# Stick-breaking attention of a trunk kernel: the next pair's scores ahead of head A's values, fillers divided about both, and suffix sums of all heads from running sums over key blocks

## What is computed

```python
z = jnp.einsum('bhqd,bhkd->bhqk', qi, k).astype(jnp.float32) * scale
strict = key_pos[None, :] < q_pos[:, None]
log_1m = jnp.where(strict, jax.nn.log_sigmoid(-z), 0.0)
tail = lax.cumsum(log_1m, axis=3, reverse=True) - log_1m
a = jnp.where(strict, jnp.exp(jax.nn.log_sigmoid(z) + tail), 0.0)
return jnp.einsum('bhqk,bhkd->bhqd', a.astype(v.dtype), v)
```

## Time and profile before

| what | value |
|---|---|
| median of three runs | 748.08 us (746.58 to 751.45) |
| the profiled execution | 748.02 us, of which the span is 746.3 us |
| busy: PE, DVE, ACT | 694.2 us (93%), 520.1 us (70%), 404.6 us (54%) |
| mean granted clock of PE | 0.978 of full speed |
| the eight heads' suffix sums and values | from 110.45 to 196.18 us |

### The profile page before, as it was taken

The page is one execution under the profiler, slowest core; times in us unless marked ns, Lnnn a source line. Parts: engine busy times, 40 slices in busy tenths (PEclk is TensorE's granted clock), DMA queues, the critical chain, the costliest instruction groups (busy, mean ns, idle before and its releaser), DMA issues.

```text
span 746.3 us, 9922 instructions
## 1 busy us (share of the span) xinstructions
PE 694.2 (93%) x3547; PEld 579.3 (78%) x3547; DVE 520.1 (70%) x567; ACT 404.6 (54%) x416; POOL 109.5 (15%) x112
## 2 busy tenths in 40 slices
PE   4999999999999999999999989999999999999920
PEld 3798889788888888888889758888888888888810
DVE  5868775868607062350745679999999999999927
ACT  6726674567414032221503337777777777777712
POOL 5000000000000000000000140333333333331120
PEclk9999999999999999999999999999999999999975
DMA  8662321000052332332592379999999999999344
GB/s 270 190 170 57 113 74 40 4 25 15 30 162 77 113 98 74 119 103 91 191 364 116 141 277 393 396 386 372 362 379 375 375 373 364 372 376 373 156 183 183
DMA packets 85169, 155.47 MB, mean 208 GB/s; under 512 B 6229, under 2 KB 37071, under 8 KB 84628
## 3 DMA queue, kind: packets, MB, share of 16 engines
q1 hardware_dynamic: 78452, 137.39, 52.2%
q0 software_dynamic: 6688, 17.69, 6.2%
HBM read 150.64 MB, written 12.58 MB: 219 GB/s over the span
## 4 chain that ended last, share of the span: by engine, by line
PE 86%; DVE 7%; ACT 3%; issue 2%; DMA 2%; POOL 1%; POOLq 0%; DVEq 0%; ACTq 0%
PE ps L483 25%; PE ps L485 24%; PE ps L484 24%; PE ps L1520 2%; PE ps L1265 1%; PE ps L1267 1%; PE ps L1446 1%; PE ps L1577 1%; PE ps L1546 1%; PE ps L1474 1%; PE ps L1303 1%; DMA y_rows<-ye,y_col 1%; DMA y_in<-y_rows 1%; DVE x L2162 1%; DVE soft_lo L1817 1%
## 5 line engine op out<-in xcount | busy, mean ns | idle before, releaser
L456 DVE TENSOR_TENSOR ring_lo<-raw_a,ring_hi 128x2048 fp32r<-128x2048 f32 (+2 forms) x58 | 115.5, 1995 | 95.8 <-ACT ring_hi L450 95.8
L456 DVE TENSOR_TENSOR ring_lo<-raw,ring_hi 128x2048 fp32r<-128x2048 f32 x71 | 161.4, 2290 | 12.3 <-ACT ring_hi L450 11.0
L450 ACT ACTIVATE ring_hi<-raw 128x2048 fp32r<-128x2048 f32 x71 | 136.3, 1920 | 19.8 <-PE ps L485 19.8
L483 PE MATMUL ps<-hT_hi,ring_hi 128*128 128x512 f32 x288 | 113.6, 394 | 2.1 <-DVE hT_lo L1667 1.8
L450 ACT ACTIVATE ring_hi<-raw_a 128x2048 fp32r<-128x2048 f32 (+2 forms) x58 | 97.4, 1680 | 32.4 <-PE ps L485 32.2
L485 PE MATMUL ps<-hT_hi,ring_lo 128*128 128x512 f32 x288 | 112.2, 390 | 0.0
L484 PE MATMUL ps<-hT_lo,ring_hi 128*128 128x512 f32 x288 | 112.2, 390 | 0.0
L483 PE MATMUL ps<-ring_hi,xT_hi 128*128 128x512 f32 x240 | 94.8, 395 | 1.8 <-DVE xT_lo L2020 1.8
L485 PE MATMUL ps<-ring_hi,xT_lo 128*128 128x512 f32 x240 | 93.8, 391 | 0.0
L484 PE MATMUL ps<-ring_lo,xT_hi 128*128 128x512 f32 x240 | 93.6, 390 | 0.0
L483 PEld LDWEIGHTS ps<-hT_hi,ring_hi 128*128 128x128 f32 x288 | 54.1, 188 | 14.4 <-DVE ring_lo L1662 1.2
(11 more groups left out here) (344 smaller groups left out, 1215.8 us busy)
## 6 DMA issues: line engine op xcount, KB each, us to landing
raw<-in_w_down SPq DMA_DIRECT2D x25, 1024.0 KB
raw<-in_w_gate SPq DMA_DIRECT2D x47, 512.0 KB
raw<-in_w_up SPq DMA_DIRECT2D x47, 512.0 KB
raw_a<-in_w_in SPq DMA_DIRECT2D x15, 1024.0 KB
raw_a<-in_w_gate SPq DMA_DIRECT2D x17, 512.0 KB
raw_a<-in_w_up SPq DMA_DIRECT2D x17, 512.0 KB
raw_a<-in_w_down SPq DMA_DIRECT2D x7, 1024.0 KB
raw_a<-in_w_in SPq DMA_DIRECT2D x10, 512.0 KB, 8.2
```

The source lines that it names most:

```text
L450: act.activation(ring_hi[:, c[0] % SPLIT, 0:width], buf[:, 0:width], ACT.Copy).then_inc(hi_ready, 1)
L456: dve.tensor_tensor(ring_lo[:, s, 0:width], buf[:, 0:width], ring_hi[:, s, 0:width].bitcast(F32), ALU.subtract).then_inc(lo_ready, 1)
L483: pe.matmul(out_ap, l_hi, r_hi, start=start, stop=False, skip_group_check=True)
```

## The change

**PE.** `tails` goes only over a key block's own block and the next one, 7 pairs, 14 matmuls. The next block is met by a new constant `negrest`, -1 where `negtri` is 0. The order becomes: `tails(A)`, three quarters of `fill_a`, `tails(B)`, the last quarter, scores of the next pair, `values(A)`, half of `fill_b`, `values(B)`, the other half. The last pair is written out apart from the loop. **DVE.** After `softplus` three additions, each linked to the one before it, add the strip of block `sbk+1` to that of `sbk`, for 2, 1 and 0: 128, 256 and 384 columns. `softplus(B+2)` now stands ahead of `value_sum(B)` and `qk_lo`. **ACT.** The Abs is a step of its own (`magnitude`), `weigh(B)` goes ahead of the copy of `fill_a`'s result, the Abs of A+2 ahead of `value_x(A)`, and the three steps of B+2 follow at once on those of A+2. `negrest` lies where `gain_rows` lay, which is read once at the start.

The diff, cut to its core:

```diff
+    negrest = sb("negrest", [P, P], F32R, "const", cursor["const"] - 512)
...
+        SUMMED = tuple(range(HEADS))
...
+            def magnitude(n):
+
+                act.wait_ge(z_ps, n + 1)
+                act.activation(soft[n % 2][:, :], scores(n), ACT.Abs).then_inc(act_c, 1)
+
             def logarithm(n):
 
-                act.wait_ge(z_ps, n + 1)
                 buf = soft[n % 2]
-                act.activation(buf[:, :], scores(n), ACT.Abs).then_inc(act_c, 1)
                 act.wait_ge(act_c, 2 * n + 1)
...
             for p in range(HEADS // 2):
                 a, b = 2 * p, 2 * p + 1
                 weigh(a)
+                if p in (1, 2):
+                    split_hi(act, K(C_MERGE + p - 1))
+                weigh(b)
                 if p == 0:
                     v_hi_part(2, 6)
                 if p == 1:
                     qk_hi(6, 6)
-                    split_hi(act, K(C_MERGE))
                 if p == 2:
                     v_hi_part(3, 6)
-                    split_hi(act, K(C_MERGE + 1))
-                weigh(b)
+                if p < HEADS // 2 - 1:
+                    magnitude(a + 2)
                 value_x(a)
                 if p < HEADS // 2 - 1:
                     logarithm(a + 2)
+                    magnitude(b + 2)
+                    logarithm(b + 2)
                 value_x(b)
                 if p == 0:
                     qk_hi(5, 6)
                 if p == 1:
                     qk_hi(7, 6)
-                if p < HEADS // 2 - 1:
-                    logarithm(b + 2)
                 value_hi(a)
                 value_hi(b)
...
-                    pe.wait_ge(consts_r, 3)
+                    pe.wait_ge(consts_r, 4)
...
                 for sbk in range(TB):
-                    for jb in range(sbk, TB):
+                    end = min(sbk + 2, TB) if n in SUMMED else TB
+                    for jb in range(sbk, end):
                         o = ZOFF[sbk] + (jb - sbk) * P
                         j, w = ZOFF[jb], ZN[jb]
-                        lhs = negtri if jb == sbk else negones
+                        lhs = negtri if jb == sbk else negrest if n in SUMMED else negones
...
-            for p in range(HEADS // 2):
+            for p in range(HEADS // 2 - 1):
                 tails(2 * p)
-                fill_a(p)
+                fill_a(p, 0, 6)
                 tails(2 * p + 1)
+                fill_a(p, 6, KD)
+                scores_pair(p + 1)
                 values(2 * p)
-                if p < HEADS // 2 - 1:
-                    scores_pair(p + 1)
-                    fill_b(p, 0, CUT)
-                else:
-                    gate_half(0, 1, 0, None, 5, KD).then_inc(chunk_used, 1)
+                fill_b(p, 0, 4)
                 values(2 * p + 1)
-                if p < HEADS // 2 - 1:
-                    fill_b(p, CUT, KD)
+                fill_b(p, 4, KD)
+            tails(HEADS - 2)
+            pe.wait_ge(av_sum, HEADS - 2)
+            gate_half(0, 1, 0, None, 0, 5)
+            tails(HEADS - 1)
+            values(HEADS - 2)
+            gate_half(0, 1, 0, None, 5, KD).then_inc(chunk_used, 1)
+            values(HEADS - 1)
...
+            dve.tensor_scalar(negrest[:, :], tri_f[:, :], -1.0, -1.0, ALU.mult, ALU.add).then_inc(consts_r, 1)
...
             def softplus(n):
                 dve.wait_ge(z_ln, n + 1)
-                dve.scalar_tensor_tensor(soft[n % 2][:, :], bank(3 * (n % 2), 3)[:, 0:ZW], 0.0, soft[n % 2][:, :],
-                                         ALU.max, ALU.add).then_inc(z_soft, 1)
+                buf = soft[n % 2]
+                ins = dve.scalar_tensor_tensor(buf[:, :], bank(3 * (n % 2), 3)[:, 0:ZW], 0.0, buf[:, :],
+                                               ALU.max, ALU.add)
+                if n in SUMMED:
+                    for sbk in (2, 1, 0):
+                        link(ins)
+                        more = buf[:, ZOFF[sbk] + P:ZOFF[sbk] + ZN[sbk]]
+                        ins = dve.tensor_tensor(more, more, buf[:, ZOFF[sbk + 1]:ZOFF[sbk + 1] + ZN[sbk + 1]], ALU.add)
+                ins.then_inc(z_soft, 1)
...
                 weight_hi(b)
                 value_sum(a)
                 weight_lo(b)
-                if p == HEADS // 2 - 1:
-                    dve.sem_inc(b_used, 3)
-                if p < HEADS // 2 - 1:
-                    softplus(a + 2)
-                    soft_split(a + 2)
+                softplus(a + 2)
+                soft_split(a + 2)
+                softplus(b + 2)
                 value_sum(b)
                 if p == 0:
                     qk_lo(5, 6)
                 if p == 1:
                     qk_lo(7, 6)
-                if p < HEADS // 2 - 1:
-                    softplus(b + 2)
                 value_lo(a)
                 value_lo(b)
```

More of the change, by code:

```diff
@@ L925, in value_hi @@
                 act.activation(sbT_hi[rows, m // 2, :], sbT_f[rows, m // 2, :], ACT.Copy).then_inc(av_h, 1)
+            magnitude(0)
             logarithm(0)
@@ L931, in _ @@
             cross_o(1)
+            magnitude(1)
             logarithm(1)
@@ L1197, in project_qk, with project_v @@
                     ins.then_inc(chunk_used if n % 2 else q_ps, 1)
-            def project_v(i, b):
+            def project_v(i, b, s0=0, s1=2 * KD):
                 wh, wl = chunk(K(C_V[i // 2]))
-                for u in range(2):
+                for step in range(s0, s1):
+                    u, k = step // KD, step % KD
                     t = 2 * (i % 2) + u
[L1204 to L1208, removed]
+                    ins = three(pe, bank(b)[:, u * 256:(u + 1) * 256], hT_hi[:, k, t * P:(t + 1) * P],
+                                hT_lo[:, k, t * P:(t + 1) * P], wh[:, k * 256:(k + 1) * 256],
+                                wl[:, k * 256:(k + 1) * 256], k == 0, k == KD - 1)
+                if s1 == 2 * KD:
+                    ins.then_inc(chunk_used if i % 2 else v_ps, 1)
             cross_scores(0)
@@ L1267, in tails @@
                         ins = pe.matmul(zz[:, o:o + w], lhs[:, :], soft_lo[n % 2][:, j:j + w], start=False,
-                                        stop=jb == TB - 1, skip_group_check=True)
+                                        stop=jb == end - 1, skip_group_check=True)
                 ins.then_inc(tail_ps, 1)
@@ L1326, in _, with fill_a @@
             project_qk(4, 6)
-            CUT = 2
-            def fill_a(p):
+            def fill_a(p, k0, k1):
                 if p == 0:
                     pe.wait_ge(qk_l, 5)
-                    project_v(2, 6)
+                    project_v(2, 6, 2 * k0, 2 * k1)
                 if p == 1:
                     pe.wait_ge(qk_l, 6)
-                    project_qk(6, 6)
+                    project_qk(6, 6, k0, k1)
                 if p == 2:
                     pe.wait_ge(qk_l, 8)
[L1338 to L1341, removed]
+                    project_v(3, 6, 2 * k0, 2 * k1)
             def fill_b(p, k0, k1):
@@ L1848, in _ @@
                 weight_lo(a)
+                if p in (1, 2):
+                    split_lo(dve, K(C_MERGE + p - 1))
                 if p == 0:
@@ L1869, in _ @@
                     qk_lo(7, 6)
-                if p < HEADS // 2 - 1:
-                    softplus(b + 2)
                 value_lo(a)
                 value_lo(b)
+            a, b = HEADS - 2, HEADS - 1
+            soft_split(b)
+            weight_hi(a)
+            weight_lo(a)
+            weight_hi(b)
+            weight_lo(b)
+            dve.sem_inc(b_used, 3)
+            value_sum(a)
+            value_sum(b)
+            value_lo(a)
+            value_lo(b)
             with dve.Fori(0, KD // 2) as dp:
```

2 lines of the change are left out of this document (removed).

## The result

The changed kernel takes 754.71 us (median of four runs, 753.34 to 756.63) against 748.12 us: ratio 1.0085, 95% interval 1.0052 to 1.0118. It is slower by 6.6 us; the forecast was +1.4 us and a range that ends at 753.5. The profiled execution took 756.63 us, the longest of the four, 8.6 us more than that of before. One later execution of the kernel before, beside the experiments, took 2985.88 us and counts in no ratio.

What follows compares the result with a forecast made beforehand. PE was taken as the bound (86% of the chain). Removing 4.6 us of PE work while waits rise from 7.2 to about 13.2 gave -2.3 + 0.8 + 1.1 + 1.8 = +1.4 us: 749.5 us, range 743.5 to 753.5.

Steps and rivals of the forecast that it cites:

- The walk: Step-by-step timing of the PE, ACT and DVE queues through one head-pair period and both ends: +1.4 us in all.
- suffix sums of a head: On PE, a head's suffix sums shrink from 2.73 to 2.15 us, 0.58 us less a head.
- wait before `values(B)`: PE, after `values(A)` and half a filler, newly waits 0.5 us for `attn_lo` of B.
- wait before suffix sums of A: PE waits 1.5 us for head A's split softplus, where it was 1.1 to 1.3.
- filler behind them: PE's filler after A's suffix sums newly waits 2.0 us for `qk_lo`, twice in the loop; 1.3 at the last pair.
- end of `values(7)`: End of the last head's values on PE, forecast near 197.6 us.
- the schedule alone: Whole forecast change from work and waits: -2.3 + 0.8 + 1.1 + 1.8 = +1.4 us.
- first end: Stretch from 110.45 us to the first new scores: 10.6 us against 12.85, so -2.3 us.
- the rival on PE's clock: Waits thin PE out and its clock falls, 1.4 us each; all six waits give 757.7 us; chance 0.08.
- A second step: Stages after 200 us: nothing moves, PE goes straight into the gates, and the experts' transfers shift with it.
- The first rival: PE waits don't grow: -4.6 us, 743.4, chance 0.17; with old waits halved -8.3, 739.7, chance 0.05.
- dearer additions: DVE's three additions cost 1.7 us a head: +2.3 us, 751.8; chance 0.12.

Runs made afterwards that it cites:

- the extra matmuls in one place: Changed kernel with 14 extra 256-column matmuls at the end of the suffix sums of head 2 only: 750.89 us, ratio 1.0037.
- new order alone: Changed kernel with the new order on all engines but no running sums (20 suffix-sum matmuls a head, no additions on DVE): 745.07 us, ratio 0.9972.
- new order, short suffix sums, no additions: Changed kernel with 14 suffix-sum matmuls a head but without DVE's three additions, leaving out the further key blocks: 741.95 us, ratio 0.9927.
- new order, long suffix sums, DVE's operations: Changed kernel with all 20 suffix-sum matmuls and three DVE maximum operations of the additions' size that change nothing: 756.22 us, ratio 1.0116.
- old DVE order: Changed kernel with `value_sum(B)` and `qk_lo` ahead of the odd softplus on DVE, as before: 747.49 us, ratio 0.9995.
- sums of odd heads: Changed kernel with running sums for the odd heads alone; even heads keep 20 suffix-sum matmuls and no additions: 746.51 us, ratio 0.9971.
- sums of odd heads on POOL: Changed kernel with running sums for odd heads alone, their three additions made by POOL instead of DVE: 744.19 us, ratio 0.9945.
- sums of heads 0 and 7: Changed kernel with running sums for heads 0 and 7 alone: 745.13 us, ratio 0.9958.
- sums in the old order: Kernel before in its old order, with running sums for all heads (14 matmuls a head, three additions): 752.07 us, ratio 1.0064.
- extra matmuls in both waits: Changed kernel with 14 extra 256-column matmuls at the end of the suffix sums of heads 2 and 4: 748.46 us, ratio 1.0000.
- the plain shift of 5.0 us: Kernel before with 22 extra 512-column matmuls between the attention stretch and the gates: 754.83 us, ratio 1.0075.

## Why the prediction was wrong

The walk, step by step, against the trace:

| step | forecast | measured |
|---|---|---|
| suffix sums of a head | 2.15 us | 2.05 us |
| additions | 0.29, 0.42, 0.56 us | 292, 425, 558 ns |
| wait before `values(B)` | 0.5 us | 0.17 us beside 0.3 of late start |
| wait before suffix sums of A | 1.5 us | 1.19 us beside 0.3 of late start |
| filler behind them | 2.0, 2.0, 1.3 us | 1.93, 1.93, 1.20 us |
| end of `values(7)` | 197.6 us | 201.07 us with two falls, 197.99 us without (the extra matmuls in one place) |
| the schedule alone | +1.4 us | +1.8 us: 748.28 us without a fall against before's 746.5 |

A row counts a wait from the end of the matmul before it, whose duration overlaps; by start to start each is 0.2 to 0.3 us longer, the late start of the table. So what the prediction says of the queues came true within 0.2 us a wait and 0.4 us at the end of `values(7)`. (The terms of its first end add up to 10.5 us, not 10.6; the total of -2.3 stands.) The same walk in the other kernels, against the lowest run (before: 746.5). The falls are those of the lowest run by its mean clock, taken off at 1.6 us each:

| kernel | walk | lowest run | falls in it | without them | median |
|---|---|---|---|---|---|
| new order alone | -3.7 | -3.1 | 0 | -3.1 | 745.07 |
| new order, short suffix sums, no additions | -7.1 | -4.9 | 1 | -6.5 | 741.95 |
| new order, long suffix sums, DVE's operations | +4.2 | +6.5 | 1 | +4.9 | 756.22 |
| old DVE order | +0.4 | +0.8 | 0 | +0.8 | 747.49 |
| sums of odd heads | -2.3 | -1.8 | 0 | -1.8 | 746.51 |
| sums of odd heads on POOL | -5.0 | -3.5 | 0 | -3.5 | 744.19 |
| sums of heads 0 and 7 | -3.7 | -3.2 | 0 | -3.2 | 745.13 |
| sums in the old order | +3.0 | +4.1 | 2 | +0.9, if each cost 1.6 | 752.07 |
| extra matmuls in both waits | +1.4 | +1.8 | 0 | +1.8 | 748.46 |

But for POOL and the sums in the old order the walk is within 0.7 us.

**The step that failed** is the rival on PE's clock. It named the mechanism and the price (1.4 us a fall, 1.6 by the steps), but it got 0.08 and no term in the sum, on the ground that waits of a period left the clock at 1.00 and so did one of 1.9 us. The waits of a period are 0.89 us long, and the one of 1.80 us at 441.65 stands alone. The change puts waits of 1.19 and 1.93 us with 2.05 us of suffix sums between them. The rows could not show that this is safe, and the step said itself that the waits lie closer together, and then gave that no weight in the sum. In the profiled execution the two waits of 1.93 us brought a fall each, 3.1 us together. The rival's price for all six waits, 757.7, was too high: those of 1.2 us brought none.

The Trainium skill, "TensorE: Matmul & The Clock Gate" (Why this matters for your kernels), says to keep idle gaps between bursts short. The gaps that it warns of are longer than either of these waits, so by that row no fall was due. The trace differs: the clock was at 0.50 from 137.7 and from 165.0 us, at and behind gaps of 1.93 us, and in one execution such a gap left it at 1.00.

**A second step** failed: "After 200 us nothing moves, since PE goes straight into the gates; the experts' transfers shift with it." The work doesn't change, but the clock does. In the profiled execution the schedule (1.8), the two falls in the attention stretch (201.07 - 197.99 = 3.1) and three later falls where before had one (2 x 1.6) make 8.1 of its 8.6 us. The median lies two microseconds lower, one later fall less; the median runs have no profile, but their mean clock, 0.971 against 0.969, says the same. Whether the late start brings the later falls is likely (the plain shift of 5.0 us took 6.6, with the interval above), not shown. How many falls a given start of the stages brings, what of a wait's length and of its nearness to another counts, and why the same wait keeps the clock in one execution and loses it in another, stays open.

The first rival (the waits don't grow) was wrong, as forecast; dearer additions too. Of the two formulas for an addition that the prediction took from the Trainium skill, "VectorE: DVE Perf Modes" (The TRN2 errata — SBUF-src ops pay a fixed extra latency per instruction), the trace bears out the second, (N + 151)/0.96: an estimate of 291 ns for 128 columns, measured 292.

## What to carry to other kernels

Before moving a step, look on PE's timeline not only at the sum of the waits but at each one's length and at what lies next to it: here waits of 1.93 us behind one of 1.19, and single waits of 2.26 us, halved the clock, for about 1.6 us each time in most kernels, while no profile shows a fall at waits of 1.55 us or less in the attention stretch. If DVE's queue decides when PE goes on, put what releases PE's next filler (here `qk_lo`) ahead of the next head's long operation; that exchange of lines was worth 7.2 us, of which 1.0 is schedule. And compare kernels by their lowest runs beside the median, with each run's mean clock: the steps of 1.6 us tell schedule from clock, and a kernel whose lowest run still has a fall shows itself by the clock.

## What the runs showed of the hardware

- PE's clock fell from 2.4 to 1.2 GHz at the end of a wait or up to 1.2 us behind it, and PE's dense work then ran at half pace: from 137.7 us for a wait that ended at 137.76, from 165.0 for one that ended at 163.99, in the old order with running sums from 135.3 for one that ended at 134.10. A fall cost 1.5 to 1.7 us in the changed kernel and in before.
- A wait of 1.65 to 1.87 us at 435 to 449 us was in all fourteen profiled executions, with a fall behind it in two.
- Most executions of the same kernel differ by whole falls: 746.5, 748.2, 749.8, 751.4 us for before, with mean clocks of 0.980, 0.978, 0.976 and 0.973.
- POOL added 384 fp32 columns in 1.33 us and 256 in 0.74 us, where DVE took 0.56 and 0.43. Beside POOL's additions DVE's `sbT_lo`, which reads two operands in SBUF, took up to 1.40 us instead of 0.68; `sbT_f` and `k_lo`, which read one of theirs in PSUM, kept their 0.69.
